# Decoding the choice of one tile's experts in two parts, with new gather quotas, in a four-tile two-block kernel

## The reference, cut to what matters

```
def one(xb):
    q = (xb @ w_q).reshape(PEER_BLOCK, PEER_HEADS, 2, PEER_HALF)
    s = jnp.einsum('thjd,hjkd->thjk', q, sub_keys)
    sv, si = lax.top_k(s, PEER_TOPK)                      # 16 of 128 keys, twice per head
    cand = sv[:, :, 0, :, None] + sv[:, :, 1, None, :]
    cs, ci = lax.top_k(cand.reshape(...), PEER_TOPK)      # 16 of the sums
    i1 = jnp.take_along_axis(si[:, :, 0], ci // PEER_TOPK, axis=-1)
    i2 = jnp.take_along_axis(si[:, :, 1], ci % PEER_TOPK, axis=-1)
    eidx = i1 * PEER_N_KEYS + i2
    g = jax.nn.softmax(cs, axis=-1)
    u, v = expert_u[eidx], expert_v[eidx]
    act = jax.nn.gelu(jnp.einsum('td,thkd->thk', xb, u), approximate=False)
    return jnp.einsum('thk,thkd->td', g * act, v)
```

## Time and profile before

| | |
|---|---|
| median of three runs | 2611.59 us |
| the profiled execution | 2619.71 us |
| its span, first to last instruction | 2617.6 us |
| TensorE busy | 2231.8 us (85%) |
| VectorE busy | 1540.7 us (59%) |
| ScalarE busy | 686.2 us (26%) |
| GpSimd busy | 1015.2 us (39%) |
| moved | 869.27 MB, 332 GB/s, of which the gathers 536.94 MB |

### The profile page before, as it was taken

How to read it: one execution, slowest core, us unless ns; L and a number is a source line. 1 busy time by engine, 2 the same in 40 slices (tenths; PEclk the granted TensorE clock), 3 DMA queues, 4 the chain that set the end, 5 groups by cost and what they waited for, 6 DMA issues and landing times.

```text
span 2617.6 us, 31879 instructions
## 1 busy us (share of the span) xinstructions
PE 2231.8 (85%) x11894; PEld 1675.4 (64%) x11894; DVE 1540.7 (59%) x3675; ACT 686.2 (26%) x2063; POOL 1015.2 (39%) x1028
## 2 busy tenths in 40 slices
PE   7999889988659999799868753568979799999898
PEld 7998778987658888688534133323356555546595
DVE  3441186764798998966633678831047668676210
ACT  6662245621225555400100010011022100001220
POOL 0000003333324554445456655656644556572000
PEclk9999999999879999999889967679987899999999
DMA  6656658999778999799999989999989999998475
GB/s 232 219 210 224 251 216 331 402 373 413 297 302 306 387 395 338 288 401 414 370 361 410 368 324 362 385 358 369 382 329 342 361 400 393 415 406 319 138 285 206
DMA packets 186090, 869.27 MB, mean 332 GB/s; under 512 B 20800, under 2 KB 21056, under 8 KB 153680
## 3 DMA queue, kind: packets, MB, share of 16 engines
q0 software_dynamic: 147456, 536.94, 53.4%
q1 hardware_dynamic: 37904, 328.20, 32.4%
q10 hardware_dynamic: 576, 2.10, 0.2%
HBM read 865.06 MB, written 2.10 MB: 331 GB/s over the span
## 4 chain that ended last, share of the span: by engine, by line
PE 67%; DVE 19%; issue 5%; ACT 4%; DMA 2%; another core or an unknown queue 2%; DVEq 0%; ACTq 0%
PE ps L988 66%; DVE rows L2313 8%; DMA wr<-in_wso 1%; DVE si L1861 1%; ACT ynT L1613 1%; PE ps L1327 1%; DVE sv L1859 1%; DVE tmpx L1946 0%; DVE ci L1861 0%; DVE oh L2128 0%; DVE h L2334 0%; DVE ps L2334 0%; DVE oh L2122 0%; PE ps L1091 0%
## 5 line engine op out<-in xcount | busy, mean ns | idle before, releaser
L968 POOL DMA_INDIRECT rows<-in_pu,eidx x512 | 484.5, 946 | 986.4 <-DVE dots L2313 435.3
L2313 DVE CUSTOM_DVE_ANT_0 rows<-rows,ps 128x1024 f32<-128x1024 f32 x512 | 594.0, 1216 | 7.2 <-issue 6.6
L988 PE MATMUL ps<-uT,wr 128*128 128x128 f32 (+2 forms) x3456 | 553.9, 318 | 20.8 <-issue 10.4
L988 PEld LDWEIGHTS ps<-uT,wr 128*128 128x128 f32 x3456 | 503.7, 195 | 55.2 <-issue 17.7
L988 PE MATMUL ps<-hT,wr 128*128 128x128 f32 (+2 forms) x1600 | 371.1, 392 | 36.7 <-issue 33.4
L968 POOL DMA_INDIRECT rows<-in_pv,eidx x256 | 287.2, 1122 | 226.1 <-DVE h L2334 112.9
L988 PEld LDWEIGHTS ps<-hT,wr 128*128 128x128 f32 x1600 | 266.3, 203 | 137.7 <-issue 43.8
L968 POOL DMA_INDIRECT rows<-in_pv,eidxT x256 | 243.3, 950 | 151.2 <-issue 63.2
L988 PE MATMUL ps<-rows,wz 128*32 128x512 f32 x1024 | 207.7, 621 | 28.6 <-DMA rows<-in_pv,eidxT 18.7
L2334 DVE SCALAR_TENSOR_TENSOR h<-rows,wgt,h 128x1024 f32<-128x1024 f32 x128 | 163.7, 1279 | 7.6 <-DMA rows<-in_pv,eidx 4.1
L2334 DVE SCALAR_TENSOR_TENSOR ps<-rows,wgt,ps 128x1024 f32<-128x1024 f32 x126 | 161.7, 1283 | 5.5 <-issue 3.7
(11 more groups left out here) (411 smaller groups left out, 2841.8 us busy)
## 6 DMA issues: line engine op xcount, KB each, us to landing
wr<-in_wg SPq DMA_DIRECT2D x48, 1536.0 KB
wr<-in_wsc SPq DMA_DIRECT2D x24, 1536.0 KB
wr<-in_wso SPq DMA_DIRECT2D x24, 1536.0 KB
wr<-in_wgu SPq DMA_DIRECT2D x33, 1024.0 KB
wr<-in_wgate SPq DMA_DIRECT2D x24, 1024.0 KB
wr<-in_wqku SPq DMA_DIRECT2D x15, 1024.0 KB
wr<-in_wo SPq DMA_DIRECT2D x12, 1024.0 KB
wr<-in_wdn SPq DMA_DIRECT2D x8, 1536.0 KB
```

The lines of the kernel that those rows point to most:

```text
L968: e.indirect_dma_start(ring[i % NR], None, A[table], bass.IndirectOffsetOnAxis(ap=index[:, t, k:k + 1], axis=0)).then_inc(gathered[i % NR] ...
L988: return e.matmul(o, l, r, start=start, stop=stop, skip_group_check=True)
L2313: e.tensor_tensor_reduce(row, row, wide[:], 1.0, 0.0, MUL, ADD, dots[:, k:k + 1]).then_inc(*dve.up(*u))
```

## The change

Tile 0's choice is decoded in two parts of four heads (`PARTS`), each with its own `slots`, `sub` and `chosen` units. The first is emitted after the `top` unit of head 4. A gather of a u row waits only for the part that its index is in; v rows wait for the last part. The merge of choice 0 and mixer 1 is split: up to the end of the first part as before, after it the choice's units carry `CZ` = 0.8 and the mixer's 0.001. Both parts use one one-hot buffer. Queries and scores of choice 0 share PSUM bank 5, and until the last query the scans of mixer 1 have the banks 3 and 4 instead of 3 to 5. The staged `wq` weights move to the end of the ring's memory, and a first gather into a slot that overlaps them waits for the last score. `SX` becomes 1.9, and the quotas are set anew. The exponent of the gates and their normalising stay with the last part.

```diff
+EARLY = 1024 * NR - 3 * 2304
...
+PARTS = (((0, 4), (4, 8)), ((0, 8),), ((0, 8),), ((0, 8),))
...
-SX = 1.6
+SX = 1.9
...
+CZ = 0.8
...
-QUOTA = {('mixer', 1, 1): 17, ('mixer', 1, 2): 19, ('late', 1): 6, ('sum', 1): 26, ('mixer', 2, 0): 66, ('mixer', 2, 1): 62, ('mixer', 2, 2): 39, ('sum', 2): 82, ('query', 2): 98, ('top', 3): 65, ('attend', 0): 142, ('heads', 0): 64, ('wout', 0): 42, ('attend', 2): 20, ('heads', 2): 19, ('wout', 2): 4, ('feed', 0): 20, ('feed', 0, 0): 28, ('feed', 0, 1): 34, ('feed', 0, 2): 49, ('down', 0, 0): 35, ('down', 0, 1): 100, ('top', 2): 0, ('query', 1): 14, ('late', 2): 20, ('feed', 0, 3): 8, ('top', 0): 0, ('mixer', 1, 0): 0}
+QUOTA = {('mixer', 1, 1): 19, ('mixer', 1, 2): 21, ('late', 1): 6, ('sum', 1): 22, ('mixer', 2, 0): 58, ('mixer', 2, 1): 62, ('mixer', 2, 2): 39, ('sum', 2): 84, ('query', 2): 104, ('attend', 0): 166, ('heads', 0): 34, ('wout', 0): 44, ('attend', 2): 20, ('heads', 2): 25, ('wout', 2): 6, ('feed', 0): 14, ('feed', 0, 0): 22, ('feed', 0, 1): 30, ('feed', 0, 2): 55, ('down', 0, 0): 37, ('down', 0, 1): 152, ('query', 1): 16, ('late', 2): 16, ('feed', 0, 3): 16, ('top', 0): 2, ('top', 2): 29, ('mixer', 1, 0): 0, ('top', 1): 0, ('rest', 0): 0, ('top', 3): 36}
...
-        self.rings = {"lo": (0, 1, 2, 3), "hi": (4, 5, 6, 7), "six": (6,), "seven": (7,)}
+        self.rings = {"lo": (0, 1, 2, 3), "hi": (4, 5, 6, 7), "five": (5,)}
...
-        pl.rings.update(lo=(0, 1, 2), hi=(3, 4, 5))
+        pl.rings.update(lo=(0, 1, 2), hi=(3, 4))
...
-    banks = (("six", "seven"), ("hi", "hi"), ("lo", "hi"))[q]
+    banks = (("five", "five"), ("hi", "hi"), ("lo", "hi"))[q]
...
+            for part in range(len(PARTS[t0]) - 1):
+                if hj // 2 == PARTS[t0][part][1]:
+                    yield from decode(t0, part)
+                    pl.stage = ("rest", q)
+                    yield "part"
+    if q == 0:
+        pl.rings.update(hi=(3, 4, 5))
...
-        yield ("chosen", t)
+        yield ("chosen", t, 0)
...
+            if k and part_of(t, k) != part_of(t, k - 1):
+                yield ("chosen", t, part_of(t, k))
...
-        yield from merge(pl, (choose[0], 0.001), (mixer[1], CX))
+        first = until("part", choose[0])
+        yield from merge(pl, (first, 0.001), (mixer[1], CX), lead=first)
+        yield from merge(pl, (choose[0], CZ), (mixer[1], 0.001))
...
-        wr += [rows[:, 2304 * i:2304 * i + 2304] for i in range(3)]
+        wr += [rows[:, EARLY + 2304 * i:EARLY + 2304 * i + 2304] for i in range(3)]
...
-                w.wait_ge(*(act.at("index", t) if kind == "row" else dve.at("chosen", t)))
+                w.wait_ge(*(act.at("index", t) if kind == "row" else
+                            dve.at("chosen", t, part_of(t, k) if kind == "dot" else len(PARTS[t]) - 1)))
+                if i < NR and 1024 * (i + 1) > EARLY:
+                    w.wait_ge(*pe.at("score", 0, 15))
```

More of the change, by code:

```diff
@@ L163, in merge @@
         if next(one[1], None) is None:
+            if one[1] is lead:
+                return
             live.remove(one)
@@ L366, in plan_choose @@
         pl.add("toplast", q, t, v=1.5)
[L367 to L376, removed]
+        yield from decode(t, len(PARTS[t]) - 1)
 def plan_attend(pl, A, t0, t1):
@@ L587, in plan_experts, with part_of @@
         yield 2 if t in VPE else 4
+def part_of(t, k):
+    return next(i for i, (a, b) in enumerate(PARTS[t]) if 16 * a <= k < 16 * b)
 def make_plan(A):
@@ L976, in gpsimd @@
                     if u[0] == "chosen":
-                        chosen.add(u[2])
+                        chosen.add((u[2], u[3]))
                     else:
                         ahead = job_of[("row", u[1], u[2], 2 * u[3] + 1) if u[0] == "rows" else u] + 1 + NR
-                    while issued < min(len(jobs), ahead) and jobs[issued][1] in chosen:
+                    while issued < min(len(jobs), ahead) and needs(jobs[issued]) in chosen:
                         gather(issued)
@@ L1643, in scalar @@
                 elif kind == "slots":
-                    _, q, t = u
-                    w.wait_ge(*dve.at("softin", t))
-                    e.activation(gate[:, t, :], gate[:, t, :], ACT.Exp).then_inc(*act.up("softexp", t))
+                    _, q, t, part = u
+                    if PARTS[t][part][1] == 8:
+                        w.wait_ge(*dve.at("softin", t))
+                        e.activation(gate[:, t, :], gate[:, t, :], ACT.Exp).then_inc(*act.up("softexp", t))
                 elif kind == "qk":
@@ L2087, in vector @@
                 elif kind == "slots":
-                    _, q, t = u
+                    _, q, t, part = u
                     m = CH[q]
                     i = t - MIXERS[q][0]
-                    cx, first, rd = m["cx1"], m["cx0"], m["rd"]
+                    hs = slice(*PARTS[t][part])
+                    cx, first, rd = m["cx1"][:, hs], m["cx0"][:, hs], m["rd"]
+                    ci = m["ci"][:, i, hs]
                     gt = gate[:, t, :].rearrange("p (h k) -> p h k", h=8)
-                    unit, place, last, second = (m[f"cy{i_}"] for i_ in range(4))
+                    unit, place, last, second = (m[f"cy{i_}"][:, hs] for i_ in range(4))
@@ L2104, in vector @@
[L2104 removed]
+                    e.tensor_scalar(second, unit, 1.0, 8.0, ALU.is_equal, MUL).then_inc(*dve.up())
+                    e.tensor_scalar(first, unit, 1.0, 0.0, SUB, ALU.max).then_inc(*dve.up())
                     then()
[L2106 to L2107 removed]
+                    e.tensor_tensor(cx, place, last, SUB).then_inc(*dve.up())
@@ L2108, in vector @@
+                    e.tensor_tensor(first, first, last, ADD).then_inc(*dve.up())
                     then()
-                    e.tensor_tensor(cx[:], cx[:], second[:], ADD).then_inc(*dve.up())
-                    e.tensor_reduce(rd[:], m["cv"][:, i], AX.X, ALU.max).then_inc(*dve.up())
-                    then()
-                    e.tensor_tensor(gt, m["cv"][:, i], b3(rd[:], 16), SUB).then_inc(*dve.up("softin", t))
-                elif kind == "sub":
-                    _, q, t, j, part = u
-                    m = CH[q]
-                    i4 = m["sif"][:, t - MIXERS[q][0]].rearrange("p (h j) k -> p h j k", j=2)
-                    oh, cx = m[f"oh{j}"], m[f"cx{j}"]
-                    then()
-                    if part == 0:
-                        for hh in (0, 4):
+                    e.tensor_tensor(cx, cx, second, ADD).then_inc(*dve.up())
@@ new lines, in vector @@
+                    if PARTS[t][part][1] == 8:
+                        e.tensor_reduce(rd[:], m["cv"][:, i], AX.X, ALU.max).then_inc(*dve.up())
+                        then()
+                        e.tensor_tensor(gt, m["cv"][:, i], b3(rd[:], 16), SUB).then_inc(*dve.up("softin", t))
+                elif kind == "sub":
+                    _, q, t, j, step, part = u
+                    m = CH[q]
+                    h0, h1 = PARTS[t][part]
+                    i4 = m["sif"][:, t - MIXERS[q][0]].rearrange("p (h j) k -> p h j k", j=2)
+                    oh, cx = m["oh0" if len(PARTS[t]) > 1 else f"oh{j}"], m[f"cx{j}"]
+                    then()
+                    if step == 0:
+                        for hh in range(h0, h1, 4):
@@ L2124, in vector @@
                                             bmid(C["iota"], 64), ALU.is_equal).then_inc(*dve.up())
-                    elif part == 1:
-                        for h in range(8):
+                    elif step == 1:
+                        for h in range(h0, h1):
                             q4 = oh[:, h, :].rearrange("p (a b) -> p a b", b=16)
```

53 lines of the change are left out of this document (30 added, 23 removed).

## The result

The changed kernel took 2633.41 us, the median of 21 runs (2618.66 to 2641.03), against 2620.09 us for the kernel before in 21 runs beside it (2605.97 to 2630.93). The ratio is 1.0042, with a 95% interval of 1.0027 to 1.0057: slower by 0.42%, some 11 us. I had forecast 0.4% faster, 2602 us in a range of 2583 to 2622. The direction is wrong. (The 2611.59 us that the forecast starts from was the median of three of the 21 runs of the kernel before; measured from 2620.09 the same forecast would read 2610.

The account below looks back on a forecast made before the run. No engine is full throughout: TensorE binds the mixers, gathers mostly bind 1266 to 1905, neither binds tile 0's choice. Terms -12 + 1 + 3 - 3 + 6 - 5 = -10 us gave 2602 us from 2611.59, range 2583 to 2622.

Parts of the forecast that it names:

- What bounds the kernel: Binder changes by stage: mixers TensorE's, 1266 to 1905 mostly the gathers', choice of tile 0 neither's.
- Choice 0 in two parts, -12: At 300 to 430: spreading the decode into mixer 1 half closes TensorE's hole; ends 0 and 24 won, 12 us taken.
- The split's cost on VectorE, +1: Decode of choice 0: small slot operations run twice, 1.5 us more with the second cast, of which 1 shows.
- One bank, +3: Choice 0: queries and scores sharing one PSUM bank add round trips, 0 to 7 us, taken as 3.
- Early gathers, 0: 6 gathers move from about 396 to about 356, the rest wait for score 15; nothing added.
- Late 1 and sum 1, -3: 28 gathers instead of 32 where the DMA is at 1.01; TensorE's wait for wso goes, 3 us won.
- Mixer 2 and late 2, +6: 175 gathers instead of 187; transfers come back at 1119 to 1410; ends 0 and +16 us, +6 taken.
- Decodes of tiles 2 and 3, 0: Top 2 and top 3 quotas from 0 and 65 to 29 and 36, DMA at 0.99 already: 0.
- Attend 0, -5: 166 gathers instead of 142, heads 0 34 instead of 64; denser dots shorten POOL's wait; ends -13 and +5 us.
- SX, 0: SX 1.6 to 1.9 moves scan units later in every mixer; only tails can change, ends -3 and +4, 0 taken.
- Rival 3: Slower, +6 to +15 us: all 16 us of gathers out of mixer 2 and late 2 return at 1119 to 1410; chance 0.23.
- The sign that I had named for being wrong: Gain at 300 to 430 is there but lost again in the stretch that the gathers bind.

Follow-up runs that it names:

- h2: The split kernel with the old quotas, CZ 0.2 instead of 0.8: 2615.17 us, 0.9987 of the kernel before.
- h1: The split kernel with the old quotas, queries of choice 0 through the mixer's three banks, only scores in bank 5: 2612.90 us, 0.9984 of the kernel before.
- f4: The kernel before, decode in one piece, with the new quotas up to query 2 only: 0.9990 of the kernel before.
- g1: The changed kernel with only the decodes of tiles 2 and 3 at their old quotas: 1.0033 of the kernel before.
- i1: The kernel before with only the tail's new quotas (attention of tile 2 to the last down product): 1.0016 of the kernel before.
- i2: The kernel before with only the middle's new quotas (decodes of tiles 2 and 3, attention of tiles 0 and 1): 1.0057 of the kernel before.

## Why the prediction was wrong, point by point

In two sums: the split's terms, -12 + 1 + 3, said -8 us, and with the old quotas it gave 0 (0.9998). The quotas' terms, -3 + 6 - 5, said -2 us, and alone they cost some 10 (1.0040). The two large steps that failed are that choice 0 wins 12 us and that attend 0 wins 5.

- **What bounds the kernel**: held. Mixer steps are TensorE's and 1266 to 1905 is the gathers' on the slower chips.
- **Choice 0 in two parts, -12**: mis-sized, and it counted one side only. With the bank's share inside, the start gave 6.9 us, where the terms -12, +1 and +3 said 8. The step that failed is the sentence "a steady mixer step runs without a hole": it was read from steps in which VectorE was busy 61.79 of 76 us, and moving the second half of the decode, some 10 us, into them beside the dots took 8.3 us (h2, with no decode left in mixer 1, has it back at 96.9). The rows to see that were on the table. With both sides counted the three terms should have been about 0 together. A slip on the way changed little: at the top of head 4 five queries are still to come, not six.
- **The split's cost on VectorE, +1**: the small operations of half width run 0.19 to 0.23 us each against 0.22 to 0.29, so the second set costs some 2 us. Its price was not its length but its place.
- **One bank, +3**: two waits of 0.37 to 0.46 us per pair, 14.2 us of waits behind the copies against 4.5, of which h1 got 4 us back. The term held in size.
- **Early gathers, 0**: nothing contradicts it, but no run has them alone. The first went out at 372, not 356, and six went out ahead of score 15 as told. TensorE's stalls without a releaser fell from 3.3 to 2.6 us only.
- **Late 1 and sum 1, -3**: nothing, 115.9 us in both.
- **Mixer 2 and late 2, +6**: the front as a whole came out at 0 (f4, 0.9966 to 1.0013). The loss in this stage had another way than I told: 7.6 us in late 2 by a PSUM bank and VectorE's queue, not by late transfers, and sum 2 gave 10.4 back.
- **Decodes of tiles 2 and 3, 0**: wrong. "The DMA is at 0.99 already" said nothing on what stands in VectorE's and TensorE's queues; +10.4 in the trace. How much of that is theirs is open: g1 without them is still at 1.0033 and 129.6 us, f4 with the new front alone at 128.9, and on the fast chip the new middle adds 3 us.
- **Attend 0, -5**: wrong sign, and the largest step that failed. I took the gap of 17.01 us of the earlier trace rows for what denser dots would fill. They don't: with 166 due instead of 142 it is 17.24 us in the changed kernel and 15.6 to 17.1 in the five other traces of the slower chips with these quotas (on the fast chip neither i1 nor i2 has it). The other end, "heads 0 falls short of gathers and becomes PE's", stood at +5 and is what ran on the fast chip, +6 us by the stretches. And the sums of the quotas were formed only to heads 0 (714 for 720); one line further they are 758 for 762, and the 4 rows owed cost 4 to 10 us before tile 2's attention, in every trace with these quotas. The middle on the kernel before alone is 1.0057.
- **The tail**: no term at all. The tail has 8 gathers more ahead of the down products, where the DMA is full (1.02), and costs 1.0016 alone, by rows that reach VectorE late. What it costs in the changed kernel is not sharp (1.0018 without it, 0.9995 to 1.0042).
- **SX, 0**: held, 1.0000 alone.

Rival 3, slower, had the size about right (2622 from 2612 is +10; +11 was measured), but that is luck: its mechanism, the twelve gathers out of mixer 2 and late 2, is the front, which alone gives 0.9990. The part of it that stood up is its attention end. The sign that I had named for being wrong, the gain lost again in the stretch that the gathers bind, was not the way either: the gain of 6.9 us was gone by the end of mixer 1.

## What to carry to other kernels

In this kernel a gather is cheapest in the stage where another engine is full and the transfers have room or just fit. Moving its due time out of such a stage into one that runs at the DMA's rate made the second one longer by the whole transfer (32 us for 24 gathers), and the first shorter by less (25 us for 30). When a table of quotas is changed, form its sums up to every point where all must be done, and price every group of it, the last one too, by both stages that it touches. And work put "into the steady state" is free only if the engine that does it has room there: look at that engine's row, not at the full one's.

## What was not expected of the hardware

The same kernel took 2519.01 us on one chip and 2617 to 2629 on the others. The stretches where TensorE was full were the same (96.9 us for mixer 1 on both), those at the gathers' rate were not: attention of tiles 0 and 1 took 335 us against 367 to 375, at 406 and 409 GB/s in the rows of i1 against 377 and 379 from 1607 to 1905 in the earlier trace rows. And a stretch on this chip ran at 413 GB/s and a DMA share of 1.02, no more than the best stretches of the others (413 at 550 to 643), so the best rate seen is the same and what differs is how long it holds. Why is open. Ratios hold between such chips only as far as the kernels are bound alike on them.
